# A two-layer decoder trunk: gated-mixer branch products in three split passes, and router logits in four column groups

## The reference

```python
# mixer_sublayer: ys = four branch results (1024 x 256 each); the sum over the branches is then multiplied by w_o
for n in range(N_BRANCH):
    gate = jax.nn.sigmoid(gate_logits[..., n * D_MODEL:(n + 1) * D_MODEL])
    merged = merged + gate * (ys[n] @ w_branch[n])
return merged @ w_o

# moe_swiglu, in layer 1 alone: eight experts, the best two of each token
probs = jax.nn.softmax((t @ router_w + router_b).astype(jnp.float32), axis=-1)
top_p, top_i = lax.top_k(probs, TOP_K)
```

## Time and profile before

| | |
|---|---|
| median of 3 runs | 5431.8 us |
| the profiled execution, whole | 5433.23 us |
| its span, first to last instruction | 5431.4 us |
| mean granted clock of TensorE | 0.981 |
| busy: PE / PEld / DVE / ACT / POOL | 95% / 81% / 51% / 33% / 14% |
| gate blocks of layer 0 / layer 1 | from 455 to 968 us / 2234 to 2739 us |
| router phase | 2832 to about 2900 us |
| expert phase | from about 2900 us |

### The profile page before, as it was taken

How to read it: one execution, slowest core, us unless ns; L and a number is a source line. 1 busy time by engine, 2 the same in 40 slices (tenths; PEclk the granted TensorE clock), 3 DMA queues, 4 the chain that set the end, 5 groups by cost and what they waited for, 6 DMA issues and landing times. The chain is left out here.

```text
span 5431.4 us, 71164 instructions
## 1 busy us (share of the span) xinstructions
PE 5179.2 (95%) x29376; PEld 4400.4 (81%) x29377; DVE 2769.4 (51%) x2570; ACT 1810.1 (33%) x1615; POOL 759.6 (14%) x329
## 2 busy tenths in 40 slices
PE   7999999899999899999996999999999999999995
PEld 5777777688788667777766999989899999998985
DVE  7444367433524643433334554545675448854566
ACT  3223121222222221312123333433553336743354
POOL 1401111144444241111111000000000000000001
PEclk9999999999999999999998999999999999999997
DMA  5312134334635521121126555655785559965578
GB/s 181 102 43 61 48 92 115 113 93 133 174 97 162 171 78 55 36 68 47 54 92 220 192 186 191 201 193 193 234 300 198 188 193 335 354 207 193 191 246 304
DMA packets 812484, 859.85 MB, mean 158 GB/s; under 512 B 20018, under 2 KB 732850, under 8 KB 811826
## 3 DMA queue, kind: packets, MB, share of 16 engines
q1 hardware_dynamic: 804322, 826.35, 46.9%
q0 software_dynamic: 4608, 16.78, 0.9%
q10 hardware_dynamic: 3408, 14.68, 0.8%
HBM read 797.96 MB, written 57.67 MB: 158 GB/s over the span
## 5 line engine op out<-in xcount | busy, mean ns | idle before, releaser
L254 PE MATMUL banks<-h_hi,w_hi 128*128 128x512 f32 x2432 | 990.6, 407 | 50.5 <-DVE h_lo L735 23.9
L254 PE MATMUL banks<-e_x_hi,e_w_hi 128*128 128x256 f32 x3584 | 1015.7, 283 | 9.7 <-DVE e_w_lo L2271 9.7
L255 PE MATMUL banks<-e_x_lo,e_w_hi 128*128 128x256 f32 x3584 | 1015.3, 283 | 0.0
L256 PE MATMUL banks<-e_x_hi,e_w_lo 128*128 128x256 f32 x3584 | 1015.2, 283 | 0.0
L256 PE MATMUL banks<-h_hi,w_lo 128*128 128x512 f32 x2432 | 954.0, 392 | 0.0
L255 PE MATMUL banks<-h_lo,w_hi 128*128 128x512 f32 x2432 | 953.6, 392 | 0.0
L2271 DVE TENSOR_TENSOR e_w_lo<-e_raw,e_w_hi 128x2048 fp32r<-128x2048 f32 x340 | 763.9, 2285 | 190.7 <-ACT e_w_hi L2209 190.7
L2209 ACT ACTIVATE e_w_hi<-e_raw 128x2048 fp32r<-128x2048 f32 x340 | 647.0, 1911 | 499.2 <-PE banks L256 488.1
L254 PEld LDWEIGHTS banks<-e_x_hi,e_w_hi 128*128 128x128 f32 x3584 | 689.2, 192 | 11.2 <-DVE e_w_lo L2271 11.0
L255 PEld LDWEIGHTS banks<-e_x_lo,e_w_hi 128*128 128x128 f32 x3584 | 689.2, 192 | 0.2
L256 PEld LDWEIGHTS banks<-e_x_hi,e_w_lo 128*128 128x128 f32 x3584 | 689.2, 192 | 0.0
(11 more groups left out here) (307 smaller groups left out, 7113.9 us busy)
## 6 DMA issues: line engine op xcount, KB each, us to landing
e_raw<-in_moe_w_dram SPq DMA_DIRECT2D x510, 1024.0 KB, 5.9
w_raw<-in_ffn_w_dram SPq DMA_DIRECT2D x120, 512.0 KB, 3.8
w_raw<-in_w_in_dram SPq DMA_DIRECT2D x108, 512.0 KB, 4.0
f_ada_raw<-in_ada_w_dram SPq DMA_DIRECT2D x48, 512.0 KB, 5.0
g_ada_raw<-in_ada_w_dram SPq DMA_DIRECT2D x32, 512.0 KB, 4.0
e_io<-row_scratch SPq DMA_DIRECT2D x13, 1024.0 KB, 7.3
x_scratch<-x_res SPq DMA_DIRECT2D x24, 512.0 KB, 2.7
row_scratch<-stage SPq DMA_DIRECT2D x24, 512.0 KB, 2.6
```

Of the source, the lines that this page charges most:

```text
L254: pe.matmul(out, wh, rh, start=first, stop=False)
L255: pe.matmul(out, wh, rl, start=False, stop=False)
L256: return pe.matmul(out, wl, rh, start=False, stop=last)
```

## The change

1. For branches 1 to 3 the products go through `mm3`. ACT rounds the branch results, once per branch and half (`branch_hi`, [128, 2, 512]), when all products of the branch before are done, into the place of that branch's operand; POOL subtracts (`branch_rest`), in place. The branch weights are rounded by ACT (`branch_w_hi`, [128, 2, 128], per block, into new room of 2 KB) and split by POOL (`branch_w_rest`), in place. Branch 0 stays.
2. `x_res` is loaded as four and four tiles, not six and two.
3. The router's weights are padded with zeros to 32 columns; k goes to column group k % 4, which has its own 32 output partitions; the four sums are added by the matmul that turns the logits, against a matrix `fold` of four stacked identities, made on DVE.

```diff
 # back_phase
+    wb_hi = [m.place(f"w_br_hi{l}{b}", [P, 2, P], F32R, m.spare + b * KB) for b in range(2)]
+    wb_lo = [m.place(f"w_br_lo{l}{b}", [P, 2, P], F32R, R + (136 + b) * KB) for b in range(2)]
+    y_hi = [m.place(f"y_hi{l}{n}", [P, 2, S], F32R, R + (96 + 8 * n) * KB) for n in range(1, NBR)]
+    y_lo = [m.place(f"y_lo{l}{n}", [P, 2, S], F32R, R + (104 + 8 * n) * KB) for n in range(1, NBR)]
...
-                    for k in range(6):
+                    for k in range(4):
                         x_load(k, s.x_in0)
...
-                    for k in range(6, KT):
+                    for k in range(4, KT):
                         x_load(k, s.x_in1)
...
+            def branch_rest(n, half):
+                pool.wait_ge(s.y_hi, 2 * (n - 1) + half + 1)
+                pool.tensor_tensor(y_lo[n - 1][:, :, toks[half]], m.ys[:, 2 * n:2 * n + 2, toks[half]],
+                                   y_hi[n - 1][:, :, toks[half]].bitcast(F32), ALU.subtract).then_inc(s.y_lo, 1)
+
+            def branch_w_rest(j):
+                pool.wait_ge(s.br_hi, j - KT + 1)
+                pool.tensor_tensor(wb_lo[j % 2][:, :, :], wb[j % 2][:, :, :], wb_hi[j % 2][:, :, :].bitcast(F32),
+                                   ALU.subtract).then_inc(s.br_lo, 1)
+
             rest_w(0)
             for j in range(NBACK):
+                if j % KT == 0 and 0 < j < NGATE:
+                    for half in range(NHALF):
+                        branch_rest(j // KT, half)
                 if j + 1 < NBACK:
                     rest_w(j + 1)
+                if KT <= j + 1 < NGATE:
+                    branch_w_rest(j + 1)
...
                     if half == 0:
-                        pe.wait_ge((s.br0, s.br1)[b], 16 * (j // 2) + 16)
-                        if mt == 0 and n == 2:
-                            pe.wait_ge(s.y2, 2)
-                        if mt == 0 and n == 3:
-                            pe.wait_ge(s.y3, 4)
+                        if n == 0:
+                            pe.wait_ge((s.br0, s.br1)[b], 16 * (j // 2) + 16)
+                        else:
+                            pe.wait_ge(s.br_lo, j - KT + 1)
+                    if n and mt == 0:
+                        pe.wait_ge(s.y_lo, 2 * (n - 1) + half + 1)
...
+                            last = mm3(pe, m.ps[:, 2 + half, :], wb_hi[b][:, k, :], wb_lo[b][:, k, :], y_hi[n - 1][:, k, toks[half]],
+                                       y_lo[n - 1][:, k, toks[half]], k == 0, k == 1)
...
+            def branch_hi(n, half):
+                act.wait_ge(s.prods, 2 * KT * n)
+                if n == 2:
+                    act.wait_ge(s.y2, 2)
+                if n == 3:
+                    act.wait_ge(s.y3, 4)
+                act.activation(y_hi[n - 1][:, :, toks[half]], m.ys[:, 2 * n:2 * n + 2, toks[half]], ACT.Copy).then_inc(s.y_hi, 1)
+
+            def branch_w_hi(j):
+                act.wait_ge((s.br0, s.br1)[j % 2], 16 * (j // 2) + 16)
+                act.wait_ge(s.prods, 2 * j - 2)
+                act.activation(wb_hi[j % 2][:, :, :], wb[j % 2][:, :, :], ACT.Copy).then_inc(s.br_hi, 1)
...
             for j in range(NGATE):
+                if j % KT == 0 and j:
+                    for half in range(NHALF):
+                        branch_hi(j // KT, half)
                 round_w(j + 1)
                 for half in range(NHALF):
                     sigmoid(j, half)
+                    if half == 0 and KT <= j + 1 < NGATE:
+                        branch_w_hi(j + 1)
...
-            dve.wait_ge(s.x_in0, 16 * 6)
+            dve.wait_ge(s.x_in0, 16 * 4)
             for k in range(KT):
-                if k == 6:
-                    dve.wait_ge(s.x_in1, 16 * 2)
+                if k == 4:
+                    dve.wait_ge(s.x_in1, 16 * 4)
 # route_phase
+            sp.wait_ge(s.padded, 2)
+            sp.dma_start(rw[:, :, 0:NE], a.router_w[e].rearrange("(k p) n -> p k n", p=P)).then_inc(s.w_in, 16)
+            sp.dma_start(rb[0:NE, :], a.router_b[e].rearrange("(n o) -> n o", o=1)).then_inc(s.w_in, 16)
...
+            pool.memset(rw[:, :, :], 0.0).then_inc(s.padded, 1)
+            pool.memset(rb[:, :], 0.0).then_inc(s.padded, 1)
...
-                    last = pe.matmul(m.ps[0:NE, 6 + half, :], rw[:, k, :], m.h_f[:, k, half * HALF:(half + 1) * HALF],
-                                     start=(k == 0), stop=(k == KT - 1))
+                    g = k % groups
+                    last = pe.matmul(m.ps[GR * g:GR * (g + 1), 6 + half, :], rw[:, k, :],
+                                     m.h_f[:, k, half * HALF:(half + 1) * HALF], start=k < groups, stop=k >= KT - groups)
...
+            pe.wait_ge(s.folded, 1)
             for t in range(ST):
-                last = pe.transpose(m.ps[:, 5, NE * t:NE * t + NE], lgt[:, P * t:P * t + P], cst[0:NE, K_ID:K_ID + NE])
+                last = pe.matmul(m.ps[:, 5, NE * t:NE * t + NE], lgt[:, P * t:P * t + P], fold[:, 0, :], start=True, stop=True)
...
+            corner = cst[:, K_ID:K_ID + P].rearrange("p (g n) -> p g n", g=groups)[:, :, 0:NE]
+            chain(dve.tensor_tensor(fold[:, 2:4, :], corner[:, 0:2, :], corner[:, 2:4, :], ALU.add))
+            dve.tensor_tensor(fold[:, 0, :], fold[:, 2, :], fold[:, 3, :], ALU.add).then_inc(s.folded, 1)
```

## The result

| | before | after |
|---|---|---|
| median | 5431.8 us | 5403.95 us (5 runs, 5401.88 to 5407.44) |
| the profiled execution, whole / span | 5433.23 / 5431.4 | 5407.44 / 5405.6 |

The ratio is 0.9949, 95% interval 0.9935 to 0.9962: 27.9 us less, where 32.8 were forecast. The profiled execution of after is the slowest of its five, 3.5 us over the median.

The account below looks back on a forecast made before the run. PE, busy 95% of the span, was taken as the bound. The terms -33.6 - 1.3 + 2.5 + 2.4 + 1.0 + 4.3 - 3.0 - 5.1 = -32.8 us, against the median 5431.8, gave 5399 us, range 5386 to 5412.

Parts of the forecast that it names:

- Products: Gate blocks, branches 1 to 3: six passes replace four float32 records, 96 products gain 0.35 each, -33.6 us; layer 1 another -1.3.
- The hand-over to branch 2 in layer 0: Layer 0, g = 31 to 33: PE's new wait falls into its existing wait for DVE; three gains lost, +1.0 us.
- The rival of a shared port: POOL's added work delays DVE's additions, PE waits 0.6 us more in all 48 blocks: 5428 us, no change; chance 0.07.
- The last branch of layer 0: PE, made faster, waits 0.6 us for DVE's conditioning sum in each of seven blocks: +4.3 us.
- The hand-over in layer 1: At branch 2, PE waits for POOL's subtraction of the branch result, +2.5 us, then runs at a slowed clock, +2.4 us.
- x: Layer 0, loads of x as four and four: shorter wait, -3.0 us; PE still waits some 2.8, its clock falls as before.
- The router: Router phase: overlapping column groups end the logits 6.7 us earlier, turning them costs 1.6 more; -5.1 us.
- The rival of serial column groups: Router: the column groups run one after another, the -6.7 us is lost and the +1.6 stays: 5406 us; chance 0.11.
- The slower rival: All 48 gate blocks: ACT stops for the branch weights' load, the sigmoid comes late; 5447 us at one microsecond each; chance 0.03.

Follow-up runs that it names:

- experiment 8: The changed kernel run again unchanged, a single run: 5399.38 us.
- experiment 9: The changed kernel run a third time unchanged, a single run: 5404.22 us.
- experiment 1: The changed kernel with branch 2's hand-over made at block 14 instead of 16, its rounded part in a free place: 5397.06 us, ratio to before 0.9935.
- experiment 4: The changed kernel with POOL filling branch 2's low part with zeros instead of subtracting: 5399.42 us, a single run.
- experiment 7: The kernel before, plus POOL subtracting branch 2's y from itself at g = 32 into memory nobody reads: 5437.11 us to 5430.78, ratio 1.001.
- experiment 3: The changed kernel with the edits of experiment 1 and experiment 2 together: 5391.41 us, ratio to before 0.9926.
- experiment 2: The changed kernel with DVE's conditioning pieces put before the rest of the merged sum in the last branch: 5397.84 us, ratio to before 0.9938.
- experiment 5: The kernel before with only the loads of x split four and four, not six and two: 5428.37 us to 5431.56, ratio 0.9997.

## Why the prediction came out as it did

The forecast of 5399 us was 5 us too low. Part of that closeness is luck: the steps missed by 9 to 11 us one way and by 2.4 to 6.6 the other.

- **Products: right.** 0.31 us per product where it stands beside small work (1.71 less 1.40), 0.33 to 0.35 per half by the sigmoids, against the 0.35 and 0.39 forecast. The six passes are not 0.227 but about 0.232 us apart. In layer 1, g = 33 to 63, 30 halves gave 10.4 us and not 11.7, and the whole of the products is 96 x 0.34 = 32.6 rather than 34.9: 2.3 us of the miss.
- **The hand-over to branch 2 in layer 0: the step that failed.** The prediction wrote "That moment doesn't move, and the gains of g = 31 to 33 are lost: +1.0 us". The wait was put in the right place, but PE's wait was taken as the whole price, and DVE's chain as fixed. The chain began 6.44 us earlier than before and should have ended that much earlier; POOL's new work, which I had costed only by PE's need of it, and the old `w_lo` that the late chain ran into took 5.93 of that from DVE. Measured: 6.8 to 9.3 us (after and experiments 8 and 9; experiments 1, 4 and 7 for the cause). That is 6 to 8 us of the miss. Not all of it is POOL. By its own numbers the prediction had this wait grow from 2.01 to 3.0 us, and it put no half clock behind it, though it did behind 2.5 and 2.8. Experiments 1 and 3, where POOL's work is out of the way, have just that wait (2.94 and 2.95) and a lowered clock behind it, and the hand-over still costs 4.1 and 2.6 us, not 1.0. The rival of a shared port had the mechanism, yet spread over 48 blocks at 0.6 us; POOL's added work cost PE time at one place, beside the tightest chain.
- **The last branch of layer 0: right**, with its mechanism: seven waits of 0.43 to 0.46 us, and 4.2 us gone by experiment 2, against 4.3. By the sigmoids the branch lost 5.1 us of its gains; the other 0.9, in every second half, stays in experiment 2, and its cause is open. The Trainium skill's rule (SBUF, "SBUF: two separate sides") is that whoever starts first holds the port for its whole instruction. The trace agrees: POOL was first by 0.05 us in the block shown, and the addition took 2.89 us. The prediction left this order open and put DVE first by 0.06, with the addition at +2.28 us from the product. That was a slip: 909.71 - 907.00 - 0.35 is 2.36, behind POOL's +2.34, so its own rows already had POOL first.
- **The hand-over in layer 1: right in its mechanism, over in its size.** The wait was 2.38 us (2.5 forecast), the clock behind it cost about 1.5 us once and nothing twice (2.4 forecast): 4.2, 2.7 and 2.7 in the three runs, against 4.9.
- **x: right in its wait** (5.85 to 3.54), **wrong on the clock in two runs of three**. With it full the gain is 4.6 us in after, else 3.1 (experiment 5), against 3.0.
- **The router: right.** PE's logits end 1.96 us after ACT's last h (2 forecast), a gain of 6.5; turning them costs 1.85 us where it was 0.66 (forecast 2.2). The phase gave 6.5 us (19.6 to 26.0), against 5.1. About 0.9 of that is a table load of ACT that DVE's softmax now waits for 0.32 us and not 1.27. The rival of serial column groups fell: 32 records in 10.19 us are 0.32 apiece, less than the 0.43 that such a record takes alone. The Trainium skill (TensorE: Matmul & The Clock Gate, "The mechanism") says that a weight load overlaps running matmuls only when the row group differs. All of these records use the full 128 rows, so by that rule they would come one after another; neither this trace nor the earlier trace rows agrees.
- **The slower rival** (ACT stopped at `w_br`) left no trace: PE never waits for the branch weights' subtraction, and no idle time of ACT ends with the load of `w_br`.

The account: -32.8 forecast; the hand-over in layer 0 adds 6 to 8, the products' spacing 2.3, the last branch 0.8; layer 1's hand-over takes back 1 to 2, the router 1.4, x up to 1.6. The end of layer 1, which the sum didn't have, takes back up to 1.6 more: the same wait of 2.14 us had half the clock behind it in the profile before and all of it after. That gives -24 to -30 us; -27.9 was measured.

What stays open: what decides the clock behind a wait of 2.1 to 4.2 us. The same kernel had it both ways (experiments 8 and 9), so no reading of one profile fixes the hand-over in layer 0 to better than 2.5 us.

## What to carry to other kernels

An engine that looks idle is not free: before work is put on POOL, look at which of DVE's operations with two SBUF inputs run beside it, and whether PE waits for that chain. A pair of subtractions (4.2 us in experiment 7, 4.7 in after) put beside the tightest chain cost that chain 4.2 and 5.9 us; moved two blocks earlier it cost it nothing. Price a wait of PE of 2 to 4 us with and without a half clock behind it, and take the forecast's range from both.

## What the runs showed of the hardware

- **Two inputs in SBUF and POOL.** The norm's SCALAR_TENSOR_TENSOR of 128x512 takes 0.75 us alone and up to 2.88 us beside POOL's subtraction. This view of the line in after has its shortest, median and longest duration in ns:

```profile
L1564 DVE SCALAR_TENSOR_TENSOR rt_sq<-rt_out,small,rt_rstd x8: 745/1492/2878, 721.1 to 2506.8; 128x512 f32<-128x512 f32 x8
```

  Before, all eight lie between 744 and 752 ns, and so they do (745 to 754) in experiment 3. DVE's multiplications with one input in the banks keep their 0.67 to 0.69 us beside POOL. POOL is stretched as well: `w_lo` from 2.37 to 2.85 us, `w_br_lo` from 0.73 to 1.19.
- **The granted clock behind the same wait is not the same.** The four matmuls behind the 2.14 us of idle time at the end of layer 1 took 3.58 us before, and 1.95 or 1.96 in seven of the ten other profiles; in the rest it was 2.52, 2.75 and 3.56, with the wait at 2.13 or 2.14 in all eleven. In the gate blocks, `w_o` and the end of layer 1, waits of 1.3 and 2.0 us never lost the clock; of 2.1 to 4.2 us sometimes; of over 5.8 each time. A term of the sum that rests on one such row, as the earlier trace rows was used, is no more than one throw of a coin.
- **The same code moves by 2 us from one execution to the next.** The phases between the two gate stretches, which the change doesn't touch, were 2.1 us longer in after's profile and 2.7 us shorter in experiment 8's. A term below that size can be read only from a stretch of the trace, not from the whole time.
